# One more first-stage slab by seven block products, and the modulation's last product and bias moved

## The reference, cut to what matters

```python
def squared_relu_mlp(x, w1, w2):                    # x 256 x 1024, w1 1024 x 4096, w2 4096 x 1024
    return jnp.square(jax.nn.relu(x @ w1)) @ w2
...
mod = silu(c) @ ada_w[l] + ada_b[l]                 # ada_w[l] 1024 x 6144
```

## Time and profile before

| what | us |
|---|---|
| median of 3 executions | 2301.51 |
| lowest and highest of them | 2298.02, 2301.95 |
| the profiled execution, its time | 2301.41 |
| the profiled execution, its span | 2299.6 |
| feed-forward of layer 0, from the first matmul of slab 1 | about 143 to 336 |
| feed-forward of layer 1, from the first matmul of slab 1 | about 626 to 820 |

### The profile page before, as it was taken

The page is one execution under the profiler, slowest core; times in us unless marked ns, Lnnn a source line. Parts: engine busy times, 40 slices in busy tenths (PEclk is TensorE's granted clock), DMA queues, the critical chain, the costliest instruction groups (busy, mean ns, idle before and its releaser), DMA issues.

```text
span 2299.6 us, 26121 instructions
## 1 busy us (share of the span) xinstructions
PE 2265.8 (99%) x11030; PEld 1373.9 (60%) x11030; DVE 1002.3 (44%) x1985; ACT 461.4 (20%) x1034; POOL 73.8 (3%) x130
## 2 busy tenths in 40 slices
PE   9999999999999999999999999999999999999998
PEld 6568548886596459996443334336999643333342
DVE  4578656767688567653211111125764311111122
ACT  3311003257111011320221111111132121111111
POOL 2000000010100000000000000000000000000000
PEclk9999999999999999999999999999999999999999
DMA  7379725354689324256999999994435699999996
GB/s 293 123 315 382 284 78 186 144 191 176 258 363 383 143 108 159 92 227 247 396 427 428 428 428 427 428 418 169 148 126 226 245 409 427 427 427 427 428 428 263
DMA packets 59168, 671.66 MB, mean 292 GB/s; under 512 B 7504, under 2 KB 7792, under 8 KB 18720
## 3 DMA queue, kind: packets, MB, share of 16 engines
q1 hardware_dynamic: 51888, 649.45, 68.9%
q0 software_dynamic: 7152, 20.43, 2.7%
HBM read 666.59 MB, written 3.26 MB: 291 GB/s over the span
## 4 chain that ended last, share of the span: by engine, by line
PE 83%; DMA 11%; DVE 5%; issue 1%; ACT 0%; SPq 0%; POOL 0%; DVEq 0%; POOLq 0%; ACTq 0%
PE ps L101 81%; DMA ring<-in_exp_w 6%; DVE arena L114 2%; DMA arena<-in_exp_w 2%; DVE arena L117 2%; PE ps L349 1%; DMA arena<-ssm_rows 1%; DMA ring<-in_ada_w 1%; PE ps L2850 1%; DMA ring<-in_mlp_w 1%; DVE X L117 0%; DMA ring<-in_attn_w_in 0%; PE ps L638 0%; DVE arena L110 0%; PE ps L2012 0%
## 5 line engine op out<-in xcount | busy, mean ns | idle before, releaser
L101 PE MATMUL ps<-arena 128*64 128x512 f32 (+6 forms) x4260 | 982.2, 456 | 14.7 <-DMA arena<-in_exp_w 5.5
L101 PEld LDWEIGHTS ps<-arena 128*128 128x128 f32 (+1 forms) x4260 | 487.5, 169 | 464.5 <-issue 434.6
L101 PE MATMUL ps<-ring,arena 128*64 128x512 f32 (+2 forms) x1720 | 462.4, 586 | 4.2 <-DMA ring<-in_exp_w 4.2
L101 PE MATMUL ps<-XTGB,ring 128*128 128x256 f32 (+1 forms) x2064 | 393.2, 347 | 0.0
L101 PEld LDWEIGHTS ps<-XTGB,ring 128*128 128x128 f32 x2064 | 342.1, 191 | 46.8 <-issue 10.7
L101 PEld LDWEIGHTS ps<-ring,arena 128*64 128x64 f32 (+1 forms) x1720 | 175.8, 151 | 261.2 <-issue 256.7
L122 DVE COPY arena<-ps 128x512 f32<-128x512 f32 (+5 forms) x133 | 63.3, 496 | 417.4 <-PE ps L101 298.5
L121 ACT COPY arena<-ps 128x512 f32<-128x512 f32 (+3 forms) x184 | 83.4, 472 | 691.2 <-PE ps L2850 287.4
L101 PE MATMUL ps<-XTGB,arena 128*128 128x128 f32 (+2 forms) x752 | 190.4, 407 | 0.0
L101 PE MATMUL ps<-ring,XTGB 128*128 128x512 f32 (+3 forms) x484 | 167.8, 501 | 1.1 <-DMA ring<-in_attn_w_in 1.0
L117 DVE TENSOR_TENSOR arena<-ps,arena 128x256 f32<-128x256 f32 (+5 forms) x269 | 115.1, 466 | 123.1 <-PE ps L101 92.6
(11 more groups left out here) (151 smaller groups left out, 971.9 us busy)
## 6 DMA issues: line engine op xcount, KB each, us to landing
arena<-in_exp_w SPq DMA_DIRECT2D x90, 2048.0 KB, 27.0
ring<-in_exp_w SPq DMA_DIRECT2D x68, 2048.0 KB, 27.9
ring<-in_mlp_w SPq DMA_DIRECT2D x25, 2048.0 KB, 12.2
ring<-in_ada_w SPq DMA_DIRECT2D x20, 2048.0 KB, 9.5
XTGB<-in_exp_w SPq DMA_DIRECT2D x18, 2048.0 KB, 32.9
ring<-in_ssm_w_in SPq DMA_DIRECT2D x12, 2048.0 KB, 7.6
ring<-in_w_in SPq DMA_DIRECT2D x12, 2048.0 KB, 7.9
ring<-in_gate_w SPq DMA_DIRECT2D x12, 2048.0 KB, 7.7
```

What stands on the lines that cost most here:

```text
L101: return self.e.matmul(o, lhsT=lhsT, rhs=rhs, start=start, stop=stop, skip_group_check=True)
```

## The change

Three edits. Layer 0's list gets slab 6, so that its `w1_sums` stand in front of a8 on DVE (s = 4), its `w1_results` behind a10 (s = 5), and PE takes 56 half-width matmuls in place of 32. In both layers the third modulation product moves from inside the last plain slab (slab 7, before its last quarter) to behind that slab. In both layers the bias, now `ada_out`, moves from in front of `block_sums` of slab 0 to behind it.

```diff
-            if n == 7:
-                v.wait_ge(at("ada mm", l, 2), at("ada_b", l))
-                for j in range(4):
-                    o = slice(32 * j, 32 * j + 3)
-                    v.then_inc(v.tt(modc[l][o, :], ps_of("ada", l)[o, :], ab[o, :], ALU.add), ("modc", l),
-                               ("read", "ada", l))
+
+        def ada_out(v, l, ab):
+            v.wait_ge(at("ada mm", l, 2), at("ada_b", l))
+            for j in range(4):
+                o = slice(32 * j, 32 * j + 3)
+                v.then_inc(v.tt(modc[l][o, :], ps_of("ada", l)[o, :], ab[o, :], ALU.add), ("modc", l),
+                           ("read", "ada", l))
...
-        W1_BLOCKS = (2, 4), (2, 4, 6)
+        W1_BLOCKS = (2, 4, 6), (2, 4, 6)
...
-                        gemm_f(pe, ("m1", l, s), ("m1", l, s), 4, mid=(lambda: ada_pe(pe, l, 8, acc)) if s == 7 else None)
+                        gemm_f(pe, ("m1", l, s), ("m1", l, s), 4)
...
+            ada_pe(pe, l, 8, acc)
...
             block_sums(v, l, 0, hT, sA, sB)
+            ada_out(v, l, ab)
             for s in range(1, NS):
                 block_sums(v, l, s, hT, sA, sB)
```

## The result

The changed kernel takes 2306.59 us (median of 20 executions, 2302.36 to 2312.22); the kernel before, in 20 executions beside it, 2298.14 us (2295.46 to 2301.95). The ratio is 1.0037, 95% interval 1.0031 to 1.0043: slower by 8.5 us. The forecast was 2308.3, 6.9 above the profiled execution. Of the three executions of the kernel before that were known then (median 2301.51), two lie at the upper end of the twenty and one, 2298.02, in their middle, so the forecast started 3.3 too high.

What follows compares the result with a forecast made beforehand. PE, busy 99% of the span, was taken as the bound. The profiled 2301.41 us plus 4.55 for net losses at S1 (+2.5 and +2.05) plus 2.35 for the clock gave 2308.3, range 2303.5 to 2311.5.

Steps and rivals of the forecast that it cites:

- The pauses: Second stage, slab 1: PE stands for S1 before its third product, 3.4 us in layer 0 and 2.8 in layer 1.
- DVE in layer 0: Slab 6's sums and results add 7.3 us on DVE, 5.0 come through; a11 ends at 239.4, PE waits 0.5.
- The round trip: From the bias's end through the write of mod to S1's start: 9.33 us in layer 0, 9.12 in layer 1.
- layer 1's +2.05: Layer 1, PE reaching S1 in slab 1: stands 2.8 us from 738.35, before it passed at 739.1; net +2.05.
- layer 0's +2.5: Layer 0, PE reaching S1 in slab 1: stands 3.4 us from 255.85, before it passed at 256.8; net +2.5.
- The clock: Behind the two new PE pauses the clock may drop, costing 0 to 3.0 us each; taken as 2.35 together.
- two drops in three: Odds that a new PE pause is followed by the low clock, at 1.75 us a drop, so 1.2 per pause.
- The strict reading: Skill's rule that the low clock follows each of the two new PE pauses; the sum would end at 2309.5.
- The rival of the quick write: With DVE idle mod's write is quick, S1 begins 4.8 us behind the bias, no PE pause: 2299.7; chance 0.12.
- the row it named itself: Test in the changed profile: DVE's pause before S1 of 5 us or less confirms the quick write, some 9 the forecast.
- What slab 6 gains: Layer 0, first stage: slab 6 by blocks takes PE 12.51 us instead of 13.97, so slab 7 ends 1.46 earlier.
- its gain of 0.75 in layer 1: Third modulation product behind slab 7 removes PE's 0.63 wait for a11; second stage begins at 722.9 instead of 723.66.

Runs made afterwards that it cites:

- e1: Changed kernel with the sums of odd slabs in the memory of the finished first-stage sums and no wait for mod: 2298.29 us, ratio 0.9999.
- e2: Changed kernel with the bias between S0 and T0 in both layers: 2297.11 us, ratio 0.9990.
- e4: Changed kernel with SP holding the loads of w2 slabs 3 to 7 until mod has landed: 2297.13 us, ratio 0.9995.
- e3: Changed kernel with slab 6 of layer 0 plain again, the two moves kept: 2305.87 us, ratio 1.0031.
- e6: Changed kernel with the third modulation product inside slab 7 again, slab 6 by blocks and late bias kept: 2301.94 us, ratio 1.0015.
- e7: Changed kernel with the bias in front of S0 again: 2299.48 us, ratio 1.0000.
- e8: Kernel before with one edit, the bias behind S0 and T0: 2298.43 us, ratio 1.0002.
- e5: Changed kernel with three unused matmuls on constants before the third product of slab 1 in both layers: 2305.31 us, ratio 1.0026.

## Why the prediction was right

**The mechanism** is the one forecast, at its place and in both layers: bias behind T0, write of mod behind the bias, S1 behind the write, PE two products into slab 1. e1 takes the dependence away and the loss with it, e2 the distance, e4 the length of the write; e3, e6, e7 and e8 show which edits are needed for it. **The pauses** were forecast at 3.4 and 2.8 and are 3.19 and 3.81.

**The base.** Part of the nearness of 2308.3 to 2306.59 is luck: the base of 2301.41 was 3.3 above the median of twenty, and the rise of 6.9 was 1.6 short of the 8.45 measured; the two errors have opposite signs.

**DVE in layer 0.** The forecast had a11 end at 239.4 and PE wait 0.5 for it; a11 ended at 238.39, and the third modulation product began at 238.63 with no pause. a10's load took the 7.6 of a lone load, as assumed. All of the difference was there before the change began to act: a7 ended 1.0 earlier in this execution (the weight sums of slab 6 begin at 205.67, not 206.7). The chain's length from there agrees to 0.1.

**The round trip** was taken as the 9.33 and 9.12 of the kernel before. From the bias's end (start + 2.87) to S1 it was 247.39 to 256.90, 9.51, and 733.93 to 744.10, 10.17. That 1.05 in layer 1 is the largest mis-sized term of the sum without the clock. By e5's stages, where the clock stays up, layer 1's +2.05 is 3.07 (with a round trip of 9.83 there) and layer 0's +2.5 is 2.27.

**The clock** was the weakest step, priced at 2.35 by two drops in three. In the profiled execution both pauses were followed by the low clock, for 4.58. The odds rested on an incomplete count: the trace of the kernel before has a fourth pause between 2 and 5 us, of 2.76 before 1440.97, and behind it the clock was low.

```profile
1438.21:1440.97 2.76, 0.00 (x0) 0.92 1.06 451
1440.97:1443.50 2.53, 2.53 (x6) 0.50 0.99 421
```

In the profiles of all ten kernels the new pauses of 3 us and more, two in the changed kernel, two in e3, one in e6, were each followed by it, five of five, and so was the one of 4.0 to 4.8 between 1550 and 1568 that every profile has. Of the 23 pauses of 2.0 to 2.8 us eleven were. So for pauses as long as those measured two in three was too low, though the forecast's own 2.8 lay where it is about one in two. The median is 8.45 above and not 9.92, and the executions spread over 10 us where those of the kernel before spread over 6.5. The spread goes with the clock: its mean over the execution is 0.996 in the three fastest of the twenty and 0.992 to 0.993 in the three slowest. At which pauses it differs the record doesn't say.

The Trainium skill, "TensorE: Matmul & The Clock Gate", Part 1, has the low clock as the default that activity releases; the five pauses agree. The strict reading, by which every pause is followed by it, doesn't hold: twelve of the 23 shorter ones weren't. By that reading the clock's term would have been 3.5, nearer to the 4.58 measured than the 2.35 taken.

**The rival of the quick write** fell by the row it named itself: DVE was idle and the write took 9.5 and 10.2. Its reading of the kernel before, that the write landed 3 us behind DVE's last sum, was a coincidence. The rule of the Trainium skill, "SBUF — State Buffer", section "SBUF: two separate sides", on the ports that DVE and GpSimd share, plays no part that these runs can see. The rival was right in one thing: the write is quick when nothing is in its way, 3.66 and 3.38 from the bias's end to S1 in e4 where the rival reckoned 4.8; but what is in its way are the weight loads, not DVE.

**What slab 6 gains**, 1.46 us, is real once nothing eats it: layer 0 is 1.10 to 1.30 shorter in e1, e2 and e4, and layer 1, without its wait for a11, 0.70. The forecast put its gain of 0.75 in layer 1 down to the move of the third modulation product, and that isn't shown: layer 1 is as short in e6 and e8 (193.75 and 193.74), where the product stands inside slab 7 and PE doesn't wait for a11 either. The wait of 0.63 in the one profile of the kernel before may be that execution's.

## What to carry to other kernels

A wait that costs nothing is covered by other work, and a move can use that cover up: before moving an operation behind others, follow what its result starts (here four additions, a write to memory, and a buffer that others wait to overwrite) to the engine that sets the time, and compare with when that engine arrives. A small transfer is priced by the queue it meets, so take its duration from a moment with the same loads on their way. If memory is free, cut such a dependence by another place for the buffer; if not, put the starter of the round trip first among the operations that may stand in any order.

## What the runs showed of the hardware

Where S1 stands right behind the bias on DVE, the same four small writes held it up for 9.25 to 10.21 us while 2 MB weight loads were queued (the changed kernel, e3, e5, e6, e8), and for 3.4 to 3.7 without them (e4). The write doesn't need all the loads to end: in layer 0 of the changed kernel it landed, and S1 began at 256.90, with the DMA engines still full. In layer 1 it was still not in when the loads had ended: in the table by stretch the last 2 us before S1 show the DMA engines (0.05) and all others idle. The two stretches:

```profile
255.00:257.00 2.00, 0.32 (x1) 0.00 (x0) 0.10 (x1) 0.00 (x0) 0.00 (x0) 1.00 0.97 412
...
742.00:744.10 2.10, 0.00 (x0) 0.00 (x0) 0.00 (x0) 0.00 (x0) 0.00 (x0) 1.00 0.05 19
```

What fills those 2 us the runs don't say; one of these writes took 1.6 to 1.9 from issue to landing in e4, about as long. The Trainium skill, "DMA: Bandwidth & Descriptors", section "Queues, rings and completion order", states that a completion count lands only after every earlier write of that DMA engine, across its queues, which would tie the small write to the loads; no run here separates that from a plain wait in line.

Pauses of PE of 3.19 and 3.81 us cost 1.6 and 3.0 more by the clock behind them in the two layers, half to four fifths of the pause itself, and three useless matmuls in the pause take that part away (e5).
